# Modulation columns of a two-layer transformer block: partition sums partly on VectorE, TensorE folding the rest four times

## The reference

```python
mod = (c @ w_ada + b_ada)[:, None, :]            # c: 1024, w_ada: 1024 x 6144
sh_m, sc_m, g_m, sh_f, sc_f, g_f = jnp.split(mod, 6, axis=-1)
h = rms_norm(x) * (1 + sc_m) + sh_m
x = x + g_m * (y @ w_out)
h = rms_norm(x) * (1 + sc_f) + sh_f
x = x + g_f * ((jax.nn.silu(gate) * up) @ w_ffn_out)
```

## Time and profile before

| | |
|---|---|
| median of 3 runs | 2962.48 us (2961.51 to 2967.85) |
| profiled execution: time, span | 2965.43 us, 2963.7 us |
| TensorE busy | 2797.8 us, 94% |
| VectorE busy | 1494.1 us, 50% |
| ScalarE busy | 958.4 us, 32% |
| mean granted TensorE clock | 0.976 |
| layer 0 | from the start to about 780 us |
| layer 1 | from about 780 to about 1500 us |
| third layer, its experts | from about 1500 us; experts from about 1766 us to the end |

### The profile page before, as it was taken

The page is one execution under the profiler, slowest core; times in us unless marked ns, Lnnn a source line. Parts: engine busy times, 40 slices in busy tenths (PEclk is TensorE's granted clock), DMA queues, the critical chain, the costliest instruction groups (busy, mean ns, idle before and its releaser), DMA issues.

```text
span 2963.7 us, 38992 instructions
## 1 busy us (share of the span) xinstructions
PE 2797.8 (94%) x12792; PEld 1677.9 (57%) x12792; DVE 1494.1 (50%) x2997; ACT 958.4 (32%) x1805; POOL 116.1 (4%) x171
## 2 busy tenths in 40 slices
PE   7899999999999999999999989999999999999997
PEld 5686678888778667888877763332323322322222
DVE  5874766765684554334375544334333433333335
ACT  4734442222473434222333422322222222222221
POOL 0000000000000003000020000000000000000002
PEclk8999999999999999999999979999999999999999
DMA  8271346764323025342323064959889899999997
GB/s 266 71 222 32 96 118 180 220 176 136 105 67 111 17 72 146 114 128 78 103 72 105 1 235 178 403 213 410 323 325 410 322 410 410 410 410 410 410 410 291
DMA packets 398913, 638.20 MB, mean 215 GB/s; under 512 B 34576, under 2 KB 284560, under 8 KB 398816
## 3 DMA queue, kind: packets, MB, share of 16 engines
q1 hardware_dynamic: 381024, 590.80, 55.5%
q0 software_dynamic: 9376, 31.14, 3.1%
q10 hardware_dynamic: 8416, 14.95, 1.4%
HBM read 610.79 MB, written 26.02 MB: 215 GB/s over the span
## 4 chain that ended last, share of the span: by engine, by line
PE 72%; DMA 10%; SPq 6%; DVE 5%; ACT 4%; issue 3%; POOL 0%; ACTq 0%; DVEq 0%; POOLq 0%
PE bank L2614 23%; PE bank L194 14%; PE bank L195 13%; PE bank L196 13%; DMA ring<-w_down 6%; SPq L2424 5%; DMA ring<-w_gate 3%; PE bank L1124 1%; PE bank L1083 1%; PE bank L1084 1%; DVE WLO L167 1%; ACT WHI L157 1%; PE bank L2608 1%; DMA ring<-w_up 1%; PE bank L1117 0%
## 5 line engine op out<-in xcount | busy, mean ns | idle before, releaser
L2614 PE MATMUL bank<-ring,xT 128*64 128x512 f32 x3200 | 731.6, 597 | 28.5 <-DMA ring<-w_up 14.8
L194 PE MATMUL bank<-HH,WHI 128*128 128x512 f32 x1344 | 543.9, 405 | 28.9 <-DVE WLO L167 12.2
L195 PE MATMUL bank<-HL,WHI 128*128 128x512 f32 x1344 | 530.9, 395 | 0.0
L196 PE MATMUL bank<-HH,WLO 128*128 128x512 f32 x1344 | 530.4, 395 | 0.0
L2614 PEld LDWEIGHTS bank<-ring,xT 128*64 128x64 f32 x3200 | 218.3, 137 | 505.2 <-issue 353.4
L2614 PE MATMUL bank<-ring,hT 128*64 128x512 f32 x1600 | 371.1, 599 | 26.7 <-DMA ring<-w_down 26.6
L167 DVE TENSOR_TENSOR WLO<-RAW,WHI 128x2048 fp32r<-128x2048 f32 (+1 forms) x132 | 281.5, 2133 | 106.4 <-ACT WHI L157 106.2
L194 PEld LDWEIGHTS bank<-HH,WHI 128*128 128x128 f32 x1344 | 257.3, 191 | 92.1 <-issue 17.6
L157 ACT ACTIVATE WHI<-RAW 128x2048 fp32r<-128x2048 f32 (+1 forms) x132 | 234.7, 1778 | 167.3 <-PE bank L196 145.9
L195 PEld LDWEIGHTS bank<-HL,WHI 128*128 128x128 f32 x1344 | 257.4, 192 | 55.0 <-issue 2.9
L196 PEld LDWEIGHTS bank<-HH,WLO 128*128 128x128 f32 x1344 | 257.0, 191 | 55.4
(11 more groups left out here) (459 smaller groups left out, 2790.6 us busy)
## 6 DMA issues: line engine op xcount, KB each, us to landing
ring<-w_gate SPq DMA_DIRECT2D x256, 512.0 KB, 9.4
ring<-w_up SPq DMA_DIRECT2D x256, 512.0 KB, 15.1
ring<-w_down SPq DMA_DIRECT2D x256, 512.0 KB, 14.8
RAW<-w_ffn_in SPq DMA_DIRECT2D x88, 512.0 KB, 5.3
RAW<-w_ada SPq DMA_DIRECT2D x40, 1024.0 KB, 5.3
RAW<-w_in SPq DMA_DIRECT2D x37, 1024.0 KB, 6.0
RAW<-w_ffn_out SPq DMA_DIRECT2D x32, 704.0 KB, 4.7
expert_results<-ysb ACTq DMA_DIRECT2D x98, 128.0 KB, 5.5
```

The source lines that it names most:

```text
L194: pe.matmul(out, lhi, rhi, start=start, stop=False)
L195: pe.matmul(out, lhi, rlo, start=False, stop=False)
L196: return pe.matmul(out, llo, rhi, start=False, stop=stop)
L2614: ins = pe.matmul(out[halves(h), :], xT[:, k % 4, halves(k // 4)], m["ring"][:, c, h * 512:(h + 1) * 512], start=False, stop=k == KD - 1)
```

## The change

In `ada()` VectorE does two more steps for each chunk. It turns `acc` in squares of 32 x 32 (partition and column swap places within each square) into the second half of the tile `acc`, and then adds up each run of 32 elements into 8 numbers, which go to row r of a new table `red` (128 x 40 x 8). So the sum over 32 partitions is made, and what stays is a sum over the four quarters of the partitions. For that a 128 x 32 matrix `fold`, four identities of 32 x 32 on top of each other, is made once from the kept identity, ahead of r = 0.

TensorE no longer has matmuls behind each chunk. At r = 8, 11, 15 and 39 alone, four matmuls with `fold` as the stationary operand and a strided piece of `red` as the moving one fill all columns that came since the last time, each matmul writing a quarter of the partitions. They are 9, 3, 4 and 24 chunks, so 18, 6, 8 and 48 columns. VectorE no longer waits for TensorE to have read `acc` (`ada_col`, r − 2). `red` and `fold` lie in a part of the tile `xpad` that is not in use between the `lru` chunks of layer 0 and of layer 1. The waits on `ada_col` 8, 11, 15 and 39 stay as they are.

```diff
--- before.py
+++ after.py
@@ -184,6 +184,8 @@
 FIRST_GROUP = first_groups()
 GROUPS = sum(GROUPS_OF[kind] for kind, _, _ in W_CHUNKS)
 assert GROUPS % 4 == 0
+
+ADA_FROM = {8: 0, 11: 9, 15: 12, 39: 16}
 
 P_AT = [0, 128, 384, 768]
 T_AT = [0, 512, 896, 1152]
@@ -555,9 +557,9 @@
         c = fed[0]
         r = L.ada.index(L.chunks[c][:2])
         v.wait_ge(*sg.event("raw", c))
-        if r >= 2:
-            v.wait_ge(*sg.event("ada_col", r - 2))
-        acc, raw = m["acc"][:, r % 2, :], m["RAW"][:, L.raw(c), :]
+        if r == 0:
+            v.tensor_reduce(m["fold"][:], K[:, K_ID:K_ID + P].rearrange("p (b c) -> p c b", c=32), AX.X, ALU.add)
+        acc, raw = m["acc"][:, 0, :], m["RAW"][:, L.raw(c), :]
         v.tensor_scalar(acc, raw[:, 0:256], m["c"][:, 0:1], None, ALU.mult).then_inc(*sg.inc("step_dve"))
         v.wait_ge(*sg.last("step_dve"))
         for k in range(1, KD):
@@ -566,6 +568,10 @@
                 ins.then_inc(*sg.inc("step_dve"))
                 v.wait_ge(*sg.last("step_dve"))
         ins.then_inc(*sg.inc("raw_used", c, also=[("ada_acc", r)]))
+        v.wait_ge(*sg.event("ada_acc", r))
+        v.transpose(m["acc"][:, 1, :], acc).then_inc(*sg.inc("step_dve"))
+        v.wait_ge(*sg.last("step_dve"))
+        v.tensor_reduce(m["red"][:, r, :], m["acc"][:, 1, :].rearrange("p (b t) -> p b t", t=32), AX.X, ALU.add).then_inc(*sg.inc("dve_out", ("red", r), also=[("ada_red", r)]))
         fed[0] += 1
 
     def feed(upto):
@@ -914,21 +920,16 @@
     def ada_columns(kind, i):
 
         r = L.ada_after.get((kind, i))
-        if r is None or (kind, i) == ("kv", 0):
+        if r not in ADA_FROM:
             return
-        which, chunk = L.ada[r]
-        if which == "own" and r == 1:
+        if r == 8:
             pe.wait_ge(*sg.event("act_out", ("lru_tanh", 3)))
-            ada_column(0)
-        ada_column(r)
-
-    def ada_column(r):
-
-        which, chunk = L.ada[r]
-        pe.wait_ge(*sg.event("ada_acc", r))
-        for j in range(2):
-            c = 2 * chunk + j
-            ins = pe.matmul(b[7 if which == "own" else 6][:, c:c + 1], m["acc"][:, r % 2, j * P:(j + 1) * P], one[:, 0:1], start=True, stop=True)
+        pe.wait_ge(*sg.event("ada_red", r))
+        rows = m["red"][:, ADA_FROM[r]:r + 1, :].rearrange("p n (j s) -> p s n j", s=4)
+        c = 2 * L.ada[ADA_FROM[r]][1]
+        out = b[6 if L.ada[r][0] == "next" else 7][:, c:c + 2 * (r + 1 - ADA_FROM[r])].rearrange("p (n j) -> p n j", j=2)
+        for t in range(4):
+            ins = pe.matmul(out[32 * t:32 * t + 32], m["fold"][:], rows[:, t], start=True, stop=True)
         ins.then_inc(*sg.inc("pe_step", also=[("ada_col", r)]))
 
     def dense(kind, i, xh=HH, xl=HL, between=None):
@@ -1285,6 +1286,8 @@
     at("mask0", 184, [P, P])
 
     at("xpad", 194, [P, 2, 516])
+    at("red", 194.25, [P, 40, 8])
+    at("fold", 195.5, [P, 32])
     at("T", 198.125, [P, S])
     at("rs", 200.125, [P, S])
     at("K", 202.125, [P, K_KEPT])
```

## The result

Four executions of the changed kernel took 2940.18 to 2945.07 us, median 2942.64; four of the kernel before beside them 2961.99. The ratio is 0.9929 [0.9917, 0.9942]: faster by 21.0 us [17.2, 24.6] of 2962. The forecast was −15.0, and the median lies just inside the range's lower end by its own figure (2942.64 against 2942.5) and just outside it by the ratio (2941). The profiled execution of after took 2940.18 us (span 2938.5, granted clock 0.979); that of before 2965.43 (2963.7, 0.976). So the two traces differ by 25.2 us, more than the medians do, and a trace of one execution has to be read with that in mind: the profiled one of after is the fastest of its four.

What follows compares the result with a forecast made beforehand. TensorE was taken as the bound, holding 72% of the chain that ended last. −16.7 (bursts) + 0.8 (folds) + 0.9 (r = 1) = −15.0 us gave a median of 2947.5 us, range 2942.5 to 2954.5.

Steps and rivals of the forecast that it cites:

- The burst: Four small matmul records on TensorE behind each modulation chunk: 0.49 us of path each, 34 removed for −16.7 us.
- VectorE's T: VectorE's added transposition and reduction per chunk: 0.92 us, bounds 0.75 and 1.5, covered by idle time nearly everywhere.
- r = 1: Modulation chunk ahead of `ga` 1, the one place where VectorE's new steps are on the path: +0.9 us (0.75 to 1.5).
- The spare time: VectorE's idle per period less the burst's 0.49: 1.90 us in `fi`, 1.29 in `fo`, to cover 0.92.
- TensorE's start of `ga` 1: Sign to look for: TensorE starts `ga` 1 near 149.4 us instead of 148.48.
- Rivals 2 to 5: 2: folds and VectorE dear, 2951.1; 3: half given back, 2955.7, 0.05; 4: nothing arrives, 2962.5, 0.04; 5: VectorE bounds, slower, 0.04.
- rival 5: VectorE becomes the bound in `fi` and `fo` if its two steps cost T: at T = 3 slower by 9.5 us; chance 0.04.
- the folds' term: Four folds on TensorE, each 0.2 us above its burst: +0.8 us, bounds +0.4 and +1.8, shape changes up to 2.0 more.
- rival 1: Clock falls ahead of `ga` 0 instead of `ga` 1: 2944.9 us; a fall elsewhere: 2950.1; within the forecast's joint 0.87.
- the own terms: What the change itself does on TensorE's path (bursts, folds, r = 1): forecast −15.0 us, −16.0 in the later trace balance.

Runs made afterwards that it cites:

- T was made 2.80: The changed kernel with VectorE's transposition and reduction made three times for each chunk: 2970.85 us, ratio 1.0025 against before.
- the changed kernels with a long one at 341.13 and at 1046.60: 341.13: after with a fold behind each chunk, 2958.22 us, 0.998; 1046.60: after with r = 1 to 6 one chunk later, 2937.75 us, 0.9918.
- after with 13 matmuls: The changed kernel with 13 unread 128 x 128 matmuls behind `gb` 0: 2950.99 us, ratio 0.9959 against before; its profiled execution took 2940.20 us.
- the second timing: The changed kernel once more, no edit, six executions: median 2942.6 us against 2964.82 for before, ratio 0.9923.

## Why the prediction was off

**Right, with sizes.** The burst: 0.49 us a chunk; the balance holds −12.76 for the `fi` and `fo` stretch where the terms make −12.84. VectorE's T: 0.93 for 0.92, 445 and 420 ns for 441 and 410. r = 1: +0.89 to +0.93 for +0.9. The spare time: 0.97 for 0.98 us in `fi`; 0.45 a chunk in `fo`, which went into catching up instead of showing as idle. TensorE's start of `ga` 1 came 0.89 us later behind the recurrence's gates, though not at "149.4": the start of the profiled execution lay 1.3 us earlier. Rivals 2 to 5 are out: folds and VectorE weren't dear, nothing was given back in the chunks, and VectorE became the bound when T was made 2.80. (Two readings of rival 5 are off: for T = 2.6 the transposition would have to be not three but nearly five times its 0.44, and 20 `fi` chunks carry a modulation chunk, not 17. Neither touches the forecast.)

**Wrong: the folds' term.** Under "What is added on TensorE" the four folds were to cost 0.8 us (bounds 0.4 and 1.8, plus up to 2.0 for changes of shape). They cost 3 × 0.39 + 0.49 = 1.66, the four bursts that they replace, by the same reckoning, 4 × 0.46 = 1.82: −0.2. The step took the busy time of eight records, 0.59 or 0.95 in its rows, as their price; the folds themselves were busy for 0.25 to 0.36 us each, and the path pays the stretch between the large matmuls on either side. 1.0 us of the gap. The Trainium skill, TensorEngine Tiling (Array Packing), Key Properties, says that a change of tiling mode drains TensorE. A cost of its own is not to be seen here: the kernel with 39 folds, 78 changes of shape, paid 0.43 us for each fold, the changes in it.

**Wrong: the clock, rival 1's size.** The mechanism stood there, but as one place worth 2.6 us of either sign, and it was left out of the sum. In fact it acts at each later stop, and in the traces the places came to −1.70, −1.63, −1.61, −0.63 and −0.98 with +0.53, −0.63, +0.79 between: −5.9 us together. That is the step that failed: many small stops behind an edit that moves them all form one term, and its size is that of the sum over the stops, here 0.5 to 1.7 us each, not of one fall. A bound of ±6, known only from this result, would have put 2941 in the range. That in the traces the clock does it, and not the edit, is shown by before with 0.9 us more work, which has all its bursts and the short stop at 343.64; by the changed kernels with a long one at 341.13 and at 1046.60; and by the granted clock beside them. That it came out as a gain is where this kernel's stops happened to lie: no row of before told it. And the trace of after with 13 matmuls had the clock fall in the hole ahead of `ga` 0 and was the better for it up to `uq`, which rival 1's "a longer hole can only lose" leaves out.

**What stays open.** The medians are off the own terms by 5.0 us (21.0 − 16.0; with the intervals 1.2 to 8.6) and 6.8 in the second timing, the traces by 9.2. Both profiled executions of after are the fastest of their timing, so the −5.9 is no measure of the medians' surplus. Over 60 executions of before in three timings the time falls by some 3 us for each 0.001 of mean granted clock (2968.5 us at 0.976, 2963.2 at 0.978, 2957.0 at 0.980). At equal mean clock the ten executions of after lie 18 to 21 us below before. So 2 to 5 us beyond the own terms don't show in that mean, of which one unit in its last place is 3 us; whether it is clock, the start or the experts the runs don't tell, since only profiled executions have a trace. Nor was the moment of a fall worked out: the table shows where it came, not why there.

## What to carry to other kernels

Price a small burst between large matmuls by the stretch it opens between them, never by its busy time: four records of one column cost 0.49 us, eight in a quarter of the array 0.43. An edit that moves everything behind it also moves each later stop of TensorE, so count the stops and give the range a term of either sign for them; here one stop moved by 0.5 to 1.7 us and eight together by 6; and before a gain below 0.3% is put down to an edit, run the kernel with a microsecond of unread work more. Once the path's own work is cut, TensorE's stops are worth filling: moving six chunks on VectorE and unread matmuls at the norms gave together 12 to 14 us, more than half of what the change gave.

## What the runs showed of the hardware that was not expected

- More work, less time: four unread matmuls of 128 x 128 (0.9 us) made before 0.8 us faster by the medians, 3.6 by the ratio and 2.6 by the spans of the traces.
- A stop of the same 1.64 us cost 1.6 to 1.7 us or nothing, by its moment: eight matmuls of 4.0 to 4.1 us at 1.2 GHz or 2.42 at 2.4.
- One kernel's executions differ by 11 us (2940.20 against 2948.68 to 2951.63), the mean clock being 0.980 in the first and 0.976 to 0.978 in the others; before's go from 2954.07 at 0.981 to 2971.13 at 0.977. The Trainium skill, TensorE: Matmul & The Clock Gate, Part 1, says that how many matmuls run at the low clock differs between executions of one kernel, and puts the loss below 1% of a kernel. What the executions differ by agrees in size: 17 us of 2960, 0.6%, but nearly as much as the whole change. The loss itself no run here isolates.
- Transposition in 32 x 32 squares costs VectorE 445 ns for 256 columns, on the line between 204 ns (32) and 711 (512), and a reduction of 256 elements 420 ns whether to one result or to eight.
